# A two-block transformer kernel on one core: keys after the query left out, gate quarters and latent attention put in another order

## What is computed

```python
x = layer_norm(ALPHA * x + h, ln_g[i, 0], ln_b[i, 0])
x = layer_norm(ALPHA * x + sq_relu_mlp(x, mlp_w1[i], mlp_w2[i]), ln_g[i, 1], ln_b[i, 1])
x = x + jax.nn.sigmoid(x @ ple_w_gate[i]) * (p[i] @ ple_w_proj[i])
```

```python
s = jnp.where(key_chunk[None, :] <= q_chunk[:, None], s, -jnp.inf)   # MLA; 128 queries a block
pr = jax.nn.softmax(s, axis=-1)
```

## Time and profile before

| | us |
|---|---|
| median of 3 runs | 2133.34 (2132.72 to 2137.8) |
| the profiled execution | 2134.08 |
| its span, first to last instruction | 2132.2 |
| PE busy | 1947.2 (91%) |
| DVE busy | 1234.3 (58%) |
| ACT busy | 903.6 (42%) |
| POOL busy | 592.7 (28%) |

### The profile page before, as it was taken

The page is one execution under the profiler, slowest core; times in us unless marked ns, Lnnn a source line. Parts: engine busy times, 40 slices in busy tenths (PEclk is TensorE's granted clock), DMA queues, the critical chain, the costliest instruction groups (busy, mean ns, idle before and its releaser), DMA issues.

```text
span 2132.2 us, 27587 instructions
## 1 busy us (share of the span) xinstructions
PE 1947.2 (91%) x11184; PEld 1701.0 (80%) x11184; DVE 1234.3 (58%) x2094; ACT 903.6 (42%) x969; POOL 592.7 (28%) x132
## 2 busy tenths in 40 slices
PE   5999999889887988999977899989999989889998
PEld 4878877778776777899767699979899977779996
DVE  6777687866977396422664532375632375973236
ACT  4544445334543242444343344433444434344442
POOL 0000000000000000687300378700378700037870
PEclk9999999999999999999989999999999999989999
DMA  6434333434232324454431455535545533254551
GB/s 256 160 138 149 128 133 124 179 134 177 99 119 65 135 99 146 175 197 177 168 132 65 144 179 197 195 119 215 193 174 197 196 119 138 79 184 177 197 195 41
DMA packets 53110, 324.96 MB, mean 152 GB/s; under 512 B 8432, under 2 KB 11888, under 8 KB 15760
## 3 DMA queue, kind: packets, MB, share of 16 engines
q1 hardware_dynamic: 43024, 308.38, 39.2%
q10 hardware_dynamic: 9984, 15.17, 2.3%
HBM read 322.47 MB, written 1.05 MB: 152 GB/s over the span
## 4 chain that ended last, share of the span: by engine, by line
PE 70%; DVE 23%; ACT 3%; issue 3%; DMA 1%; SPq 0%; DVEq 0%; ACTq 0%
PE project L794 37%; PE output L794 26%; DVE wlo L1433 4%; DVE arena L1536 2%; DVE arena L1804 1%; DVE XTl L1885 1%; PE turn L964 1%; PE output L909 1%; PE output L931 1%; DVE st L1527 1%; ACT whi L1133 1%; DVE arena L1698 1%; DVE arena L1782 1%; PE project L1049 1%; PE project L1018 1%
## 5 line engine op out<-in xcount | busy, mean ns | idle before, releaser
L762 POOL TENSOR_TENSOR wlo<-raw,whi 128x2048 fp32r<-128x2048 f32 x128 | 592.5, 4658 | 1490.4 <-ACT whi L1133 1473.5
L1133 ACT ACTIVATE whi<-raw 128x2048 fp32r<-128x2048 f32 x291 | 554.8, 1914 | 507.7 <-PE project L794 312.8
L794 PE MATMUL project<-XTh,whi 128*128 128x256 f32 x1488 | 427.1, 287 | 10.1 <-DVE XTl L1885 8.8
L794 PE MATMUL project<-XTh,wlo 128*128 128x256 f32 x1488 | 425.0, 286 | 0.0
L794 PE MATMUL project<-XTl,whi 128*128 128x256 f32 x1488 | 424.8, 286 | 0.0
L1433 DVE TENSOR_TENSOR wlo<-raw,whi 128x2048 fp32r<-128x2048 f32 x163 | 376.1, 2321 | 65.7 <-ACT whi L1133 65.4
L2110 DVE TENSOR_TENSOR arena<-arena 128x512 f32<-128x512 f32 x64 | 144.0, 2285 | 461.3 <-ACT arena L1383 461.3
L794 PE MATMUL output<-whi,YTh 128*128 128x512 f32 x736 | 293.7, 399 | 16.4 <-DVE YTl L1885 12.0
L794 PEld LDWEIGHTS project<-XTh,whi 128*128 128x128 f32 x1488 | 289.6, 195 | 13.8 <-DVE XTl L1885 11.2
L794 PE MATMUL output<-wlo,YTh 128*128 128x512 f32 x736 | 291.5, 396 | 0.0
L794 PE MATMUL output<-whi,YTl 128*128 128x512 f32 x736 | 290.6, 395 | 0.0
(11 more groups left out here) (225 smaller groups left out, 2153.7 us busy)
## 6 DMA issues: line engine op xcount, KB each, us to landing
raw<-in_units SPq DMA_DIRECT2D x291, 1024.0 KB, 4.8
arena<-in_ln_g ACTq DMA_DIRECT2D x8, 512.0 KB, 3.9
arena<-in_ln_b ACTq DMA_DIRECT2D x8, 512.0 KB, 5.0
tok<-in_mem SPq DMA_DIRECT2D x2, 512.0 KB, 6.0
arena<-in_mem_norm_gain ACTq DMA_DIRECT2D x2, 512.0 KB, 4.6
arena<-in_norm_gain ACTq DMA_DIRECT2D x2, 512.0 KB, 5.6
xres<-in_x SPq DMA_DIRECT2D x1, 1024.0 KB, 14.9
arena<-in_mem ACTq DMA_DIRECT2D x1, 1024.0 KB, 6.3
```

The lines of the kernel that those rows point to most:

```text
L762: pool.tensor_tensor(wlo[:, slot, :], raw[:, slot, :], whi[:, slot, :], ALU.subtract).then_inc(lo_pool, 1)
L794: mm = pe.matmul(out, x if x_stationary else w, w if x_stationary else x, start=start and i == 0, stop=stop and i == 2, skip_group_check=True)
L1133: act.activation(whi[:, slot, :], raw[:, slot, :], ACT.Copy).then_inc(hi_done, 1)
```

## The change

1. **Late keys.** For dilated and MLA heads the first 128 queries take scores, mask, exponential, transposes and values of the first 128 keys only (`key_spans`, `key_tiles`). Memory heads are as before.
2. **Gate.** The quarters run in the order 0, 2, 1, 3. In layers 0 to 2 turn (0,0) and then turn (1,0) stand after the third of them and before the last; turn (0,1) follows the last; turn (1,1) stands inside the first unit of the next layer, which is cut into its two banks. `gate_post` of each quarter stands beside them in the list.
3. **Second layer norm.** Turn (0,0) comes before the statistics of the third quarter; turn (0,1) moves behind the whole layer norm and is late; the first `half` steps wait for two freed banks, not four.
4. **MLA.** `mlatab` moves from the start of the MLA layer into layer 0's MLP, behind its first two units. The norm of the latents is four DVE operations instead of three. The low weights of one unit and the clearing and filling of `krz` move behind the latents' turns. A head's PT comes two slots after its S, the first two S stand among the v products, and the first pair of result turns comes before the last slots.
5. **Output.** Four transfers, one a quarter, in place of one.

```diff
         def one(u, ahead=True, between=()):
+            f = dict(g=g, u=u, src=src, fm=feature_major)
+            unit("proj", (w, "P", u, col), ahead=ahead, banks=(0,) if between else (0, 1), **f)
+            if between:
+                while between:
+                    between.pop(0)()
+                add("proj", n=len(units) - 1, ahead=False, banks=(1,), **f)
...
-        for c in range(2):
-            turn("x", 0, c, "X", 4 * c)
-        if early:
-            add("ln", g=g, h=1, part=1)
-            add("ln", g=g, h=1, part="rest")
+        add("ln", g=g, h=1, part="sum", c=0)
+        turn("x", 0, 0, "X", 0)
+        add("ln", g=g, h=1, part="stat", c=0)
+        quarter(1, 1)
+        add("ln", g=g, h=1, part="rest")
+        turn("x", 0, 1, "X", 4, late=True)
...
-                              stages=["T", "S", "PT", "PV"] if kind != "mla" else ["S", "PT", "PV"]))
+                              stages=["T", "S", "PT", "PV"] if kind != "mla" else ["S", None, "PT", "PV"]))
...
     def mla():
-        add("mlatab")
         project(("mla_w_in", 0), 0, "lat")
-        unit("rope", ("mla_rope", "R", 0, 0), g=g)
+        unit("rope", ("mla_rope", "R", 0, 0), ahead=False, g=g)
         add("post", g=g, tag="krope", on="sv")
         for h in range(H2):
             turn("lat", h, 0, "Y", 8)
+        add("ahead", n=len(units) - 1)
+        add("post", g=g, tag="krz", on="v")
...
+        if i == 0:
+            add("mlatab")
         add("mlp", i=i, n=n0, g=g, q=n["q"], src_n=n["src"])
...
         if i + 1 < LAYERS2:
-            for h, c in ((0, 0), (0, 1), (1, 0)):
-                turn("x", h, c, "X", 4 * c)
-        add("qpost", g=g, post="ple", src_n=n["src"], pg=pg + 1, quarters=(3,))
+            gate_quarters(*GATE_ORDER[:3])
+            gate_post(0)
+            turn("x", 0, 0, "X", 0)
+            gate_post(1)
+            turn("x", 1, 0, "X", 0)
+            gate_quarters(GATE_ORDER[3])
+            add("ahead", n=last)
+            gate_post(2)
+            turn("x", 0, 1, "X", 4, late=True)
+            gate_post(3)
+            late.append(lambda: turn("x", 1, 1, "X", 4, late=True))
...
+        def key_spans(hd):
+            return (S, S) if hd["kind"] == "mem" else (P, S)
+        def key_tiles(hd):
+            return ((0, 0), (0, 1), (1, 1), (1, 0)) if hd["kind"] == "mem" else ((0, 0), (0, 1), (1, 1))
...
-                    pe.wait_ge(q_evac, 4 * f["g"])
+                    pe.wait_ge(q_evac, 4 * f["g"] - 2 + 2 * f["h"])
...
-            sp.dma_start(a["out"].rearrange("(h p) d -> p h d", p=P), xres[:, :, :]).then_inc(out_done, 16)
+            for k, x in enumerate(GATE_ORDER):
+                h, cs = x // 2, slice((x % 2) * 512, (x % 2 + 1) * 512)
+                sp.wait_ge(tsrc, totals["src"] + k + 1)
+                sp.dma_start(a["out"][h * P:(h + 1) * P, cs], xres[:, h, cs]).then_inc(out_done, 16)
```

More of the change, by code:

```diff
@@ L41 @@
 FF_CHUNKS = 8
+GATE_ORDER = (0, 2, 1, 3)
 TWO_PI = 2.0 * np.pi
@@ L129, in pieces, with one @@
         n["p"] += 1
-        def one(u, ahead=True):
-            unit("proj", (w, "P", u, col), ahead=ahead, g=g, u=u, src=src, fm=feature_major)
+        def one(u, ahead=True, between=()):
+            f = dict(g=g, u=u, src=src, fm=feature_major)
[4 more added lines that the diff above has]
+                add("proj", n=len(units) - 1, ahead=False, banks=(1,), **f)
         def scalar_post():
@@ L149, in project @@
         g, one, scalar_post, vector_post = pieces(w, col, tag, **f)
-        one(0)
+        one(0, between=late)
         after_unit()
-        flush()
         if between is not None:
@@ L204, in tail @@
         def tail(u):
-            unit("tail", (w, "Q", u, 0), g=g, u=u, src=src, ple=False, conv=conv)
+            unit("tail", (w, "Q", u, 0), g=g, u=u, src=src, ple=False, conv=conv, xs=range(4))
             units.append((w, "Q", u + 1, 0))
@@ L221, in layer_norm, with quarter @@
     def layer_norm(g, early):
+        def quarter(h, c):
+            add("ln", g=g, h=h, part="sum", c=c)
+            add("ln", g=g, h=h, part="stat", c=c)
         for c in range(2):
-            add("ln", g=g, h=0, part=c)
+            quarter(0, c)
         add("ln", g=g, h=0, part="rest")
-        add("ln", g=g, h=1, part=0)
         if not early:
-            add("ln", g=g, h=1, part=1)
-        for c in range(2):
-            turn("x", 0, c, "X", 4 * c)
-        if early:
-            add("ln", g=g, h=1, part=1)
-            add("ln", g=g, h=1, part="rest")
+            for c in range(2):
+                quarter(1, c)
+            for c in range(2):
+                turn("x", 0, c, "X", 4 * c)
+            return
+        add("ln", g=g, h=1, part="sum", c=0)
[4 more added lines that the diff above has]
+        turn("x", 0, 1, "X", 4, late=True)
     def quad(kind, vg, j0=0, **f):
@@ L408, in mla @@
         n["p"] += 2
+        for c in range(2):
+            quad("mla", g + c, j0=4 * c, kn=g, g=0)
         for b in range(2):
@@ L1366, in _ @@
                 elif kind == "qpost":
-                    if f["post"] == "ple" and f["quarters"][0] == 0:
-                        for x in range(4):
-                            act.wait_ge(q_done, 4 * f["g"] + x + 1)
-                            if x >= 2:
-                                act.wait_ge(tsrc, f["src_n"] + x - 1)
-                            act.activation(ple_t[:, x % 2, :], PQ[x][:, :], ACT.Tanh, scale=0.5).then_inc(q_evac, 1)
-                            last.other(q_evac, 4 * f["g"] + x + 1)
+                    if f["post"] == "ple":
+                        k = f["k"]
+                        act.wait_ge(q_done, 4 * f["g"] + k + 1)
+                        if k >= 2:
+                            act.wait_ge(tsrc, f["src_n"] + k - 1)
+                        act.activation(ple_t[:, k % 2, :], PQ[f["x"]][:, :], ACT.Tanh, scale=0.5).then_inc(q_evac, 1)
+                        last.other(q_evac, 4 * f["g"] + k + 1)
                 elif kind == "mlp":
@@ new lines, in _ @@
+                    if f["part"] == "sum":
+                        c = f["c"]
+                        x = 2 * h + c
+                        cs = slice(c * 512, (c + 1) * 512)
+                        dve.wait_ge(q_done, 4 * g + x + 1)
+                        dve.scalar_tensor_tensor(out=tok[:, h, cs], in0=xres[:, h, cs], scalar=ALPHA,
+                                                 in1=PQ[x][:, :], op0=ALU.mult, op1=ALU.add).then_inc(q_evac, 1)
+                        last.other(q_evac, 4 * g + x + 1)
+                    elif f["part"] == "stat":
+                        c = f["c"]
+                        cs = slice(c * 512, (c + 1) * 512)
+                        dve.wait_ge(q_evac, 4 * g + 2 * h + c + 1)
+                        dve.bn_stats(st[:, 16 + 6 * c:22 + 6 * c], tok[:, h, cs]).then_inc(dve_own, 1)
+                        last.own()
+                        if c == 1:
```

177 lines of the change are left out of this document (91 added, 86 removed).

## The result

| | before | after |
|---|---|---|
| median | 2133.34 (3 runs), 2137.8 with those beside it (5) | 2116.49 (5 runs, 2113.83 to 2122.47) |
| span of the profiled execution | 2132.2 | 2114.3 |
| granted clock, mean | 0.969 | 0.966 |

The ratio to the kernel before is 0.9915 (95% interval 0.989 to 0.994), 18 us of 2133 (the medians above differ by 17 and by 21): a gain clear of the noise, where the forecast was 22. The total hides what happened: the places came out from 17.6 us better to 14 us worse than before, two of them far from what the sum said.

The account below looks back on a forecast made before the run. The prediction took PE, 70% of the chain, as the bound, with DVE 23%. Seven terms summed to −21.7 us from the profiled 2134.1: 2112.4, or 2111.7 for the median, stated as 2111, range 2099 to 2119.

Parts of the forecast that it names:

- Term 3: Ends of three gates: turns between the quarters open two PE waits near 2.8 us, 27.0 us each, +6.2 us in all.
- Rival B: Gate ends run at full clock, 25.8 us each, and a gate start lacks its slow stretch: 2106 us; chance 0.15.
- Term 1: Late keys in the dilated heads: 1.4 us less a group, less one half-clock stretch, −7.7 us.
- Rival C: Dilated layer: PE, done earlier, waits longer for full DVE; 7 of 7.7 us given back, 2118 us; chance 0.10.
- Term 2: Four gate starts: nothing won, one more issue each and one half-clock stretch charged, +2.0 us.
- Term 4: Tables in layer 0's MLP: DVE operations wait beside POOL and delay the relu that PE needs, +3.0 us.
- rival A: Tables in layer 0's MLP run unhindered by POOL and cost 0: 2108 us; chance 0.18.
- rival D: Layer 0's MLP: each DVE table operation waits for a whole POOL piece, all twelve giving 2164 us; slower than before, chance 0.07.
- Terms 5 and 7: Latents: sums done earlier and work moved behind the turns, −5.0 us; output: three quarters transferred early, −1.9 us.
- Term 6: MLA heads: slots of 2.35 us with the exponential hidden, 33.8 us where 53.1 was counted before, −18.3 us.

## Why the prediction was off

The direction and the places were right, the total a little too good: 22 forecast, 18 measured (0.9915, against 0.9895 forecast). 2116.5 lies inside the range, but a ratio of 0.9915 on the 2137.8 measured beside it gives 2119.6, just past its upper end of 2119. Term 3 cost 7.8 us more than its forecast, and terms 1 and 2 gave 6.7 us more than theirs: that the total came so close is luck.

- **Term 3, gate ends, is the step that failed.** Its times at full clock were right (transposes of turn (1,0) at 11.5 from the tail's start, forecast 11.55; waits 2.74, 1.51, 2.85). I took 27.0, "25.8 to 28.1", and gave both slow stretches together at most 2.3 us. They were 10.24 us long and cost 5.1, and the part at 1.2 GHz also delays ACT, whose high weights wait for PE's progress: 30.2, 30.2, 29.5. The term was +14 for +6.2, and measured against the old gate end with the tables out of it (22.6, 22.9, 25.6) the new one costs 18.8. Rival B (full clock, 25.8) was the wrong side. What spoke for it, that waits near 1.4 us left the clock alone, was misread: 1.8 us behind the end of the wait of the earlier trace rows the trace before has 3.41 us at half clock (253.65 to 257.06).
- **Term 1 was too small**, −12.0 for −7.7. Of the 4.3 us, 2.0 is 0.4 a group: DVE's first copy of its full stretch comes 22.97 us behind the group's first transposes before and 21.86 after, 1.1 us of PE rather than 1.0, and DVE's full stretch behind it, with its narrower operations, is 0.7 us shorter (22.02 for 22.72) rather than 0.4. 1.5 is the slow stretch I charged for a longer wait; the wait grew by 0.1, and there are three stretches in the layer before and after. The rest lies in the last group and in where slow stretches fell. Rival C (the gain given back) is refuted by the groups' 43.9 us.
- **Term 2** charged a slow stretch too, +2.0 for −0.4. It went the other way: before, each of the four starts has one behind the 2.65 us wait (3.41 us, and 6.83 in the third gate, whose start took 13.5 us), and after none has. The half norm's order is otherwise neutral, as the run that undoes it shows.
- **Term 4** came out at +3.0 for the reason given: DVE done at 869.2, which is 881.4 in the time of before, forecast 881.6. Which operations would wait was open. Three did, a cast, a tensor-scalar and a tensor-tensor, each until a POOL piece ended. The Trainium skill (SBUF — State Buffer, "Who interferes with whom") names both kinds, casts and tensor-scalars in 2-port mode and operations with two SBUF inputs, and the trace agrees with it (2.77, 4.55 and 4.69 us), though no row shows the mode of an operation; rival A with its free one-input operations is refuted, and rival D's twelve blocked pieces too, since POOL made only three in that time.
- **Terms 5 and 7** held: −5.4 for −5.0, −2.0 for −1.9.
- **Term 6** held in the slot (2.34) and came out at −17.6 for −18.3. The heads took 1.8 more than the 33.8 counted, with the 13.65 us stretch at their end; one of 6.83 us behind the next layer norm (3.41 before) cost 1.7 more, and was no term at all.

Common to the misses: I priced a slow stretch by one rule, "a wait near 2.8 brings one of 3.41 us at half chance", at three places. It was too high at two and too low at the third.

## What to carry to other kernels

When an order is changed, write down for the two engines that serve PE what stands behind what: one residual behind a turn's copy, and a unit's weights ahead of a tanh, opened two long waits, and moving them (not the quarters) was worth 14 us; dropping a third wait that PE did not need, 11. Where several waits stand close together, add their slow stretches in full to a hand count made at full speed. Then check in a trace, since the same waits had them in one gate and not in the next. Put short work of DVE where POOL rests.

## What was not expected of the hardware

- **Clock behind waits.** All stretches at 1.2 GHz in these traces last 3.41, 6.83, 10.24 or 13.65 us, but for the last one of a trace, which its end cuts short. Three waits of 2.74, 1.50 and 2.85 us (2.65 in the third gate) within 10 us went with 10.24 us of it in each gate; in the first two gates 3.41 came with the second wait and 6.83 with the third, in the third gate 6.83 with the first wait and 3.41 with the third; two of 2.74 and 2.85 by none in two gates and by 10.24 us in the third; two of 1.07 and 1.41 by none, none and 6.83 us. I did not find what tells them apart.
- **The same instructions, several lengths.** Up to 840 us (layer 0's output product) the changed kernel and eleven of the others issue the same instructions but for the tables. Seven of these profiles reach that point within 0.9 us of each other, with half-clock stretches of 3.41 us at 576 and 627 us; three (gate undone, transposes one slot back, output in one piece) have 6.83 us there and one more of 6.83 at 301, and reach it 8.5 to 8.8 us later; two lie at 3.5 and 6.7. It fits the spread of one kernel's times (2113.83 to 2122.47).
- **One SBUF input can be enough to wait.** A cast of 128x256 took 2.77 us and a tensor-scalar of that size 4.55 beside POOL's subtraction, 0.29 and 0.35 without it. The layer norm's sums, which read one operand from SBUF and one from PSUM, ran at their usual 0.67 and 0.68 beside a POOL piece (843.03 to 847.65), and so did its statistics (BATCH_NORM_STATS2, one operand, from SBUF) at 0.69.
